# Solving a triangular recurrence on one Trainium2 core: VectorE transposes and half-width updates in place of matmuls

## What is computed

```python
def wkv_scan(r, w, k, v, a, b, state0, reverse):
    def step(S, inp):
        r_t, w_t, k_t, v_t, a_t, b_t = inp
        sa = jnp.einsum('bhij,bhj->bhi', S, a_t)
        S = S * w_t[:, :, None, :] + sa[..., None] * b_t[:, :, None, :] + v_t[..., None] * k_t[:, :, None, :]
        return S, jnp.einsum('bhij,bhj->bhi', S, r_t)
...
def bidir_scan(f, s0_f, s0_b):
    y_f, s_f = wkv_scan(f['r'], f['dec_f'], f['k_f'], f['v'], f['a'], f['b_f'], s0_f, False)
    y_b, s_b = wkv_scan(f['r'], f['dec_b'], f['k_b'], f['v'], f['a'], f['b_b'], s0_b, True)
    return y_f + y_b, s_f, s_b
```

## Time and profile before

| | |
|---|---|
| runs | 2574.65, 2575.28, 2576.94 us |
| span of the profiled execution, first to last instruction | 2575.0 us |
| TensorE (PE) busy, matmul records | 2536.2 us (98%), 17267 |
| weight loads (PEld) busy | 1622.8 us |
| VectorE (DVE) busy | 1176.1 us (46%), 2446 instructions |
| ScalarE (ACT) busy | 508.6 us (20%), 1057 |
| GpSimd (POOL) busy | 56.8 us |
| mean granted clock of TensorE | 0.999 |
| recurrence, 1311 to 1535 us | 224.0 us, of which PE is busy 217.2, DVE 132.3, ACT 63.5, POOL 45.8 |

### The profile page before, as it was taken

The page is one execution under the profiler, slowest core; times in us unless marked ns, Lnnn a source line. Parts: engine busy times, 40 slices in busy tenths (PEclk is TensorE's granted clock), DMA queues, the critical chain, the costliest instruction groups (busy, mean ns, idle before and its releaser), DMA issues.

```text
span 2575.0 us, 41365 instructions
## 1 busy us (share of the span) xinstructions
PE 2536.2 (98%) x17267; PEld 1622.8 (63%) x17267; DVE 1176.1 (46%) x2446; ACT 508.6 (20%) x1057; POOL 56.8 (2%) x87
## 2 busy tenths in 40 slices
PE   8999999999999999999999999999999999999998
PEld 7856888578758886587789899433433343334333
DVE  5755666566647575525566554322122222221223
ACT  1102421021113311215532234111011101110111
POOL 0010000000000000000011110000000000000000
PEclk9999999999999999999999999999999999999999
DMA  7466254454453444552300105999999999999997
GB/s 279 175 186 236 71 222 164 177 199 163 180 213 115 165 174 170 211 196 88 109 19 4 52 30 221 363 420 420 420 417 418 420 420 411 420 420 418 408 420 292
DMA packets 92079, 637.74 MB, mean 248 GB/s; under 512 B 10680, under 2 KB 10680, under 8 KB 18576
## 3 DMA queue, kind: packets, MB, share of 16 engines
q1 hardware_dynamic: 90288, 629.67, 61.3%
q0 software_dynamic: 1600, 5.38, 1.0%
HBM read 632.38 MB, written 2.62 MB: 247 GB/s over the span
## 4 chain that ended last, share of the span: by engine, by line
PE 94%; DMA 2%; DVE 1%; ACT 1%; SPq 1%; issue 0%; DVEq 0%; ACTq 0%
PE ps L1502 27%; PE ps L744 18%; PE ps L812 10%; PE ps L1001 6%; PE ps L892 4%; PE ps L1460 3%; PE ps L952 2%; DMA ring<-weights 2%; PE ps L1440 2%; PE ps L735 2%; PE ps L1260 2%; PE ps L1282 1%; PE ps L1271 1%; PE ps L1048 1%; PE ps L1400 1%; PE ps L1491 1%
## 5 line engine op out<-in xcount | busy, mean ns | idle before, releaser
L1502 PE MATMUL ps<-ring,arena 128*64 128x512 f32 (+1 forms) x1248 | 338.4, 594 | 1.1 <-ACT arena L2014 0.7
L1502 PE MATMUL ps<-arena 128*64 128x512 f32 (+1 forms) x1224 | 337.0, 594 | 1.0 <-ACT arena L2014 0.7
L1502 PEld LDWEIGHTS ps<-ring,arena 128*64 128x64 f32 (+1 forms) x1248 | 111.7, 141 | 180.5 <-issue 173.2
L1502 PEld LDWEIGHTS ps<-arena 128*64 128x64 f32 (+1 forms) x1224 | 111.9, 142 | 173.6 <-issue 167.3
L744 PE MATMUL ps<-arena 128*128 128x256 f32 x960 | 220.8, 378 | 0.0
L2864 DVE TENSOR_SCALAR X<-ps 128x256 f32<-128x256 f32 (+1 forms) x64 | 28.7, 449 | 396.1 <-PE ps L1502 396.1
L744 PEld LDWEIGHTS ps<-arena 128*128 128x128 f32 x960 | 178.1, 189 | 24.1 <-issue 0.2
L1001 PE MATMUL ps<-arena,ring 128*128 128x256 f32 x784 | 173.0, 381 | 0.0
L812 PE MATMUL ps<-arena 128*128 128x512 f32 x352 | 165.5, 592 | 0.0
L1001 PEld LDWEIGHTS ps<-arena,ring 128*128 128x128 f32 x784 | 148.0, 190 | 24.7 <-issue 5.6
L744 PE MATMUL ps<-ring,X 128*128 128x256 f32 x640 | 151.4, 380 | 0.0
(11 more groups left out here) (549 smaller groups left out, 3715.7 us busy)
## 6 DMA issues: line engine op xcount, KB each, us to landing
ring<-weights SPq DMA_DIRECT2D x366, 1024.0 KB, 7.8
arena<-weights SPq DMA_DIRECT2D x153, 1024.0 KB, 19.6
con<-weights SPq DMA_DIRECT2D x25, 1024.0 KB, 20.4
vec<-weights SPq DMA_DIRECT2D x25, 1024.0 KB, 19.8
vec<-weights SPq DMA_DIRECT2D x25, 512.0 KB, 14.9
con<-weights SPq DMA_DIRECT2D x25, 512.0 KB, 17.4
con<-consts SPq DMA_DIRECT2D x1, 1872.5 KB, 16.7
vec<-vectors SPq DMA_DIRECT2D x1, 1671.5 KB, 20.2
```

The source lines that it names most:

```text
L1502: last = mm(put(half), stationary(4 * kq + k), part[:, at:at + 512], start=False, stop=(kq == 1 and k == 3))
```

## The change

Three things are changed, all in the recurrence, and one is moved.

1. Level 0: the unit-matrix matmuls on TensorE (L1246) and the ScalarE copy (`first`) go. VectorE turns the tile itself: `v.transpose` turns each 32 by 32 block of the tile in place. Up to level 4 nothing outside the 32 by 32 blocks on the diagonal is set, so that turning the blocks turns the matrix.
2. Levels 1 to 4: `grown_turned` goes from TensorE and VectorE. After both chunks' additions VectorE turns the new Z (`turned`). Level 5, which sets entries outside these blocks, keeps its product (`last_turned`).
3. Levels 1 to 4: `chained`, the copy of W, `grown` and the addition work on the 32 columns per head that the level can change (`fresh` picks them: of each pair of column blocks of size 2^n one), not on all 64.
4. `ahead` leaves the levels of pairs 1 to 3. Tile 0 stays in pair 0's levels, parts 1 and 2 of tile Q + 1 come after pair Q's `last_turned`, and parts 3 to 5 after the first half of `begun` for pair Q + 1.

```diff
+        def fresh(a, d, n):
+            size = 1 << n
+            return a.rearrange("p (k s e) -> p k s e", s=2, e=size)[:, :, d, :]
...
-                        for x in range(2):
-                            if x:
-                                keys_turned(Q, 1)
-                            pe.wait_ge(e_ready, edge_at(Q, 0, x))
...
-                                    last = mm(ps[two(hp), (4, 5)[x], at:at + CH], XZS[x][two(hp), 1, p, :], C("eye2")[two(hp), :], start=True, stop=True)
-                            last.then_inc(d_done, 1)
+                        keys_turned(Q, 1)
...
+                                    if n < 5:
+                                        last = mm(ps[two(hp), w_bank(n, x), p * CH // 2:(p + 1) * CH // 2], EBS[x][two(hp), n % 2, p, :], fresh(XZS[x][two(hp), 0, p, :], d, n), start=True, stop=True)
...
-                                    last = mm(ps[two(hp), (5, 0)[x], p * CH:(p + 1) * CH], XZS[x][two(hp), 1, p, :], WWS[x][two(hp), p, :], start=True, stop=True)
+                                    last = mm(ps[two(hp), (5, 0)[x], p * CH // 2:(p + 1) * CH // 2], XZS[x][two(hp), 1, p, :],
+                                              WWS[x][two(hp), p // 2, (p % 2) * CH // 2:(p % 2 + 1) * CH // 2], start=True, stop=True)
...
                         for n in range(1, 6):
-                            chained(n, 0)
-                            if n > 1:
-                                grown_turned(n - 1, 1)
-                            chained(n, 1)
+                            for x in range(2):
+                                chained(n, x)
                             if n < 5:
-                                grown(n, 0)
-                                grown_turned(n, 0)
-                                grown(n, 1)
-                        grown_turned(5, 0)
+                                for x in range(2):
+                                    grown(n, x)
+                        last_turned(0)
                         inward(Q, 0)
-                        grown_turned(5, 1)
+                        last_turned(1)
...
+                                wide = 256 if n == 5 else 128
+                                A(WWS[x][:, :, :].rearrange("p a b -> p (a b)")[:, 0:wide], ps[:, w_bank(n, x), 0:wide], ACT.Copy).then_inc(w_ready, 1)
...
+                        dve.wait_ge(e_ready, edge_at(Q, 0, x))
+                        v.transpose(XZS[x][:, 0, :, :], XZS[x][:, 1, :, :]).then_inc(z_first, 1)
...
+                            xz = fresh(XZS[x][:, 0, :, :].rearrange("p a b -> p (a b)"), d, n)
+                            v.tensor_tensor(xz, xz, ps[:, (5, 0)[x], 0:128].rearrange("p (k e) -> p k e", e=1 << n), ALU.add).then_inc(xz_ready, 1)
+
+                        def turned(n, x):
+                            dve.wait_ge(xz_ready, 8 * Q + 2 * (n - 1) + x + 1)
+                            v.transpose(XZS[x][:, 1, :, :], XZS[x][:, 0, :, :]).then_inc(xt_ready, 1)
...
+                        for n in range(1, 5):
+                            for x in range(2):
+                                grown(n, x)
+                            for x in range(2):
+                                turned(n, x)
+                            if Q == 0:
+                                ahead(0, n)
+                        for x in range(2):
+                            last_turned(x)
+                        if Q == 0:
+                            ahead(0, 5)
+                        if Q < 3:
+                            ahead(Q + 1, 1)
+                            ahead(Q + 1, 2)
...
                                 begun(Q + 1, 0)
+                                if Q < 3:
+                                    for n in (3, 4, 5):
+                                        ahead(Q + 1, n)
```

More of the change, by code:

```diff
@@ L1238, in second @@
                         Q = 4 * d + m
-                        for x in range(2):
-                            if x:
-                                keys_turned(Q, 1)
-                            pe.wait_ge(e_ready, edge_at(Q, 0, x))
-                            for p in range(4):
-                                for hp in range(2):
-                                    at = p * CH
-                                    last = mm(ps[two(hp), (4, 5)[x], at:at + CH], XZS[x][two(hp), 1, p, :], C("eye2")[two(hp), :], start=True, stop=True)
-                            last.then_inc(d_done, 1)
+                        keys_turned(Q, 1)
                         def chained(n, x):
@@ L1259, in chained @@
                                 for hp in range(2):
-                                    last = mm(ps[two(hp), w_bank(n, x), p * CH:(p + 1) * CH], EBS[x][two(hp), n % 2, p, :], XZS[x][two(hp), 0, p, :], start=True, stop=True)
+                                    if n < 5:
+                                        last = mm(ps[two(hp), w_bank(n, x), p * CH // 2:(p + 1) * CH // 2], EBS[x][two(hp), n % 2, p, :], fresh(XZS[x][two(hp), 0, p, :], d, n), start=True, stop=True)
+                                    else:
+                                        last = mm(ps[two(hp), w_bank(n, x), p * CH:(p + 1) * CH], EBS[x][two(hp), n % 2, p, :], XZS[x][two(hp), 0, p, :], start=True, stop=True)
                             last.then_inc(w_done, 1)
@@ L1270, in grown, with last_turned @@
                                 for hp in range(2):
-                                    last = mm(ps[two(hp), (5, 0)[x], p * CH:(p + 1) * CH], XZS[x][two(hp), 1, p, :], WWS[x][two(hp), p, :], start=True, stop=True)
+                                    last = mm(ps[two(hp), (5, 0)[x], p * CH // 2:(p + 1) * CH // 2], XZS[x][two(hp), 1, p, :],
+                                              WWS[x][two(hp), p // 2, (p % 2) * CH // 2:(p % 2 + 1) * CH // 2], start=True, stop=True)
                             last.then_inc(d_done, 1)
-                        def grown_turned(n, x):
-                            if n == 1 and x == 0 and m:
+                        def last_turned(x):
+                            if x == 0 and m:
                                 pe.wait_ge(st_ready, 9 * d + 2 * m + 1)
-                            if n == 5:
-                                pe.wait_ge(w_ready, 10 * Q + 8 + x + 1)
-                                pe.wait_ge(xt_ready, 10 * Q + 6 + x + 1)
+                            pe.wait_ge(w_ready, 10 * Q + 8 + x + 1)
+                            pe.wait_ge(xt_ready, 10 * Q + 6 + x + 1)
                             for p in range(4):
@@ L1904, in solved @@
                         A(UU[:, :, :].rearrange("p a b -> p (a b)"), ps[:, 3, 256:512], ACT.Copy).then_inc(uu_ready, 1)
-                    def first(Q, x):
-                        act.wait_ge(d_done, 10 * Q + x + 1)
-                        A(XZS[x][:, 0, :, :], ps[:, (4, 5)[x], 0:256].rearrange("p (a b) -> p a b", a=4), ACT.Copy).then_inc(z_first, 1)
                     keys(4 * d, 0)
@@ L1912, in second @@
                         Q = 4 * d + m
-                        first(Q, 0)
                         keys(Q, 1)
-                        first(Q, 1)
                         for n in range(1, 6):
@@ L1918, in second @@
                                 act.wait_ge(w_done, 10 * Q + 2 * (n - 1) + x + 1)
-                                A(WWS[x][:, :, :].rearrange("p a b -> p (a b)"), ps[:, w_bank(n, x), 0:256], ACT.Copy).then_inc(w_ready, 1)
+                                wide = 256 if n == 5 else 128
+                                A(WWS[x][:, :, :].rearrange("p a b -> p (a b)")[:, 0:wide], ps[:, w_bank(n, x), 0:wide], ACT.Copy).then_inc(w_ready, 1)
                             if Q == 3 and n in (3, 4):
@@ L2633, in grown @@
                         def grown(n, x):
-                            dve.wait_ge(d_done, 10 * Q + 2 * n + x + 1)
+                            dve.wait_ge(d_done, 8 * Q + 2 * (n - 1) + x + 1)
                             if n == 1:
@@ new lines, in grown, with last_turned @@
+                            v.tensor_tensor(xz, xz, ps[:, (5, 0)[x], 0:128].rearrange("p (k e) -> p k e", e=1 << n), ALU.add).then_inc(xz_ready, 1)
+                        def turned(n, x):
+                            dve.wait_ge(xz_ready, 8 * Q + 2 * (n - 1) + x + 1)
+                            v.transpose(XZS[x][:, 1, :, :], XZS[x][:, 0, :, :]).then_inc(xt_ready, 1)
+                        def last_turned(x):
+                            dve.wait_ge(dt_done, 2 * Q + x + 1)
+                            dve.wait_ge(xt_ready, 10 * Q + 6 + x + 1)
@@ L2646, in grown_turned @@
                             xt = XZS[x][:, 1, :, :]
                             v.tensor_tensor(xt, xt, ps[:, (7, 2)[x], 0:256].rearrange("p (a b) -> p a b", a=4), ALU.add).then_inc(xt_ready, 1)
[L2649 to L2659, removed]
```

## The result

The changed kernel took 2589.26 us in the median (2587.5 to 2590.0, 4 runs), the kernel before 2575.06 (2574.65 to 2576.94, 4 runs): ratio 1.0051, interval 1.0038 to 1.0065. It is slower by 0.5%; the forecast was 2554.0 us. The profiled execution has a span of 2588.0 us, with a mean granted clock of 0.980 where it was 0.999.

The account below looks back on a forecast made before the run. TensorE was taken to bound the recurrence (busy 217.2 of 224.0 us). Eight pairs saving 2.5 + 0.4 us, less 0.6, 0.2 and 1.4, gave 21.0 us off 2575.0: 2554.0 us, range 2545 to 2568.

Parts of the forecast that it names:

- The clock falls: Rival: in the recurrence TensorE's granted clock drops to its 1.2 GHz level, giving 2700 us or more; chance 0.02.
- A group of half the columns: TensorE, levels 1 to 4: 16 records moving 32 columns last 0.63 us instead of 0.66, TensorE taken for 0.47.
- One level: Narrow levels of the recurrence: the chain of hand-overs ends last, at 2.09 us per level instead of 2.8.
- Levels 2 to 5: Recurrence, each pair: these levels take 7.9 us where 10.38 stood, 2.5 us less per pair.
- The start of a pair: Before level 2, where VectorE is late: 0.6 us less in short-mask pairs, taken as 0.4 per pair.
- `ahead`: Moved VectorE work before the second chunk just fits; charged 0.2 us for each of three pairs, 0.2 more in pair 0.
- The transposes: VectorE in the levels: each turn of a 128x256 tile takes 0.43 us, covered by other work.
- the addition: VectorE after each grown group: 0.29 us when narrow, against 0.42 before.
- the copy: ScalarE's copy of W in a narrow level: 0.28 us, against 0.38 for 256 columns.
- VectorE becomes the bound: Rival: a 32-bit transpose takes four passes, 1.2 us, so VectorE limits the recurrence: 2582 us; chance 0.05.
- picked columns read slowly: Rival: TensorE reads level 1's spaced column pairs at a quarter of the rate: 2597 us; chance 0.02.
- narrow groups narrower: Rival: TensorE's narrow groups in levels 1 to 4 last 0.45 us instead of 0.63: 2545 us; chance 0.08.

Follow-up runs that it names:

- e1: Changed kernel with each narrow matmul of levels 1 to 4 moving its 32 columns twice; 2556.95 us, ratio 0.9921 to the kernel before.
- e4: Changed kernel without the narrowing: levels 1 to 4 multiply, copy and add all 64 columns per head; 2562.61 us, ratio 0.9945 to the kernel before.
- e9: Changed kernel with added 32-column matmul groups that nobody reads in level 1 alone; 2568.32 us, ratio 0.9969 to the kernel before.
- e7: Changed kernel with unread 32-column matmul groups added in levels 1 to 4, level 1 filled too; 2586.51 us, ratio 1.0028 to the kernel before.
- e2: Changed kernel with unread 32-column groups added after second chained (levels 2 to 4) and second grown groups (levels 1 to 4); 2614.07 us, ratio 1.0153.
- e3: Changed kernel with unread 64-column groups added after second chained (levels 2 to 4) and second grown groups (levels 1 to 4); 2593.16 us, ratio 1.0087.
- e8: Changed kernel with narrow groups moving their columns twice and unread 64-column groups added in levels 1 to 4; 2577.53 us, ratio 1.0002.

## Why the prediction was wrong

The step that failed is in the rival *The clock falls*: "It will be busy 1.87 of 2.1, 89% again". The share was about right (5.09 of 6 us before the fall), what it was taken to mean was not. A record counts as busy whether it moves 64 columns or 32, and a stretch at 89% with 64-column groups says nothing of one with 32-column groups. e1 and the changed kernel have the same records and, where both run at full clock, nearly the same waits; they differ only in the columns, and lie 32 us apart (2556.95 and 2589.26). I gave that rival 0.02, and its price was wrong too: "2700 or more" had the clock low throughout, while it came back in every pair. By the levels, 99 us at the lower clock cost 99 x (1 - 2.16/3.41) = 36 us, an estimate; between the spans of the changed kernel and e1 lie 31.7.

The second thing missed was the stops at a pair's start. The prediction had VectorE as what is late there, but counted that only as time. The Trainium skill, TensorE: Matmul & The Clock Gate, section Why this matters for your kernels, warns of idle between bursts. The trace agrees in part: stops of 0.39 to 0.50 us in pair 5 are followed by the lower clock with narrow groups, and stops of 0.36 to 1.30 us are not with wide ones (e1, e4).

The sum nearly held at full clock. e1 has the changed kernel's work at clock 0.999, with a span of 2556.3: 18.7 us less than before, forecast 21.0. Term by term, from pair 5 of e1:

- *A group of half the columns*: 0.63 to 0.66 us in the changed kernel, forecast 0.63; TensorE is taken for 0.46 (1472.40 to 1472.86). That is 0.029 us per record. The Trainium skill's floor near 25 ns (same page, section Back-to-back issue gap) is not reached here; the measurement decides.
- *One level*: 2.21 us in e1, 2.16 narrow at full clock, forecast 2.09.
- *Levels 2 to 5*: 1453.37 to 1461.69 is 8.32, forecast 7.9, before 10.38. Over all eight pairs they took 87.9 us before and take 69.6 in e1: 18.3 less, and the forecast, with what it charged in pairs 0 and 3, was 18.4. That agreement is luck: a level is longer than forecast, but pair 5, whose 10.38 stood for all pairs, was the shortest before (the others 10.49 to 12.69).
- *The start of a pair* and *`ahead`* hold the miss: forecast 3.2 less 0.6, measured about 0.4, which is what is left of 18.7. In pair 5 the start came out as taken (3.92 us from VectorE's first instruction to level 2, 4.30 before). But from `inward` to the next pair's level 2 TensorE takes 0.2 to 0.4 us longer than before ahead of pairs 1 to 3, whose `ahead` was moved there, and 0.1 to 0.6 less ahead of pairs 4 to 7; level 1 of pair 0 takes 0.6 longer. How much of that is `ahead` was not tested.
- *The transposes*, *the addition*, *the copy*: as forecast, and no row shows anyone waiting for a transpose.
- *VectorE becomes the bound*, *picked columns read slowly*, *narrow groups narrower*: none occurred.

e4 splits the gain: transposes without narrowing give 14.3 us (2576.88 to 2562.61); narrow copies and additions give 5.7 more (e1). The narrow matmuls gave nothing, since the group's length hardly changes, and cost 32.

**The better version** is e1: 2556.95 us, ratio to before 0.9921 (0.9905 to 0.9938). It keeps the whole change and moves the 32 columns twice.

## What to carry to other kernels

When matmuls are made narrower, look at the granted clock by stage before believing the busy share: records of half the columns look just as busy. Where a narrow matmul takes TensorE no less time, move the full width anyway and narrow only what other engines copy and add. If it must be narrow, keep TensorE from stopping where the narrow groups begin (e9: 2568.32 us for 2589.26).

## What was not expected of the hardware

- Neither stops nor narrow groups lowered the clock by themselves: 64-column groups held 1.00 across stops up to 1.30 us (e1), 32-column groups held it in the six of eight pairs that ran through (e7), and the two together brought 0.50 in eight of eight (changed kernel). Whether they are two conditions, or two ways to lower one quantity, no run separates.
- Once low, the clock stayed at 0.50 with TensorE busy 10.00 of 10 us on narrow groups (e2), and the wide groups of level 5 ran at it too (1.10 us per group for 0.68).
- The fall varies between runs of one kernel: e3 took 2585.02 to 2608.72 us, e8 with wide groups only 2575.96 to 2578.61. What counts in a narrow group, and how long a stop must be, was not settled.
